# Another order of the same work in a three-layer fp32 block kernel

## The reference, cut to what matters

```python
# first block: one layer, no feed-forward
h = rms(x, norm_w) @ w_in                      # 1024 -> 3584
oa = diff_attention(rms(qa), rms(ka), va)      # 4 heads, two 64-wide maps each, softmax, w = p0 - lam * p1
orr = rms(retention_fwd + retention_bwd)       # 4 heads, decay masks, chunks of 128
x = x + concat(rms(oa) * silu(ga), orr * silu(gr)) @ w_out
# second block, layer 0: bidirectional mLSTM with 4 heads; layer 1: window attention, 16 query heads, 4 kv heads, rope
x = x + mixer(rms(x)) ; x = x + (silu(h @ Wg) * (h @ Wu)) @ Wd      # feed-forward width 2816
return rms(x) * norm_final_w
```

## Time and profile before

| | us |
|---|---|
| median of 3 runs | 1539.77 |
| lowest, highest | 1539.58, 1541.7 |
| the profiled execution | 1538.49 |
| its span (first to last instruction) | 1536.7 |
| PE busy | 1455.4 |
| DVE, ACT, POOL busy | 800.9, 595.0, 52.8 |
| mean granted TensorE clock | 0.976 |

### The profile page before, as it was taken

One profiled execution on the slowest core, in us unless ns is written; L12 is line 12 of the kernel. 1 busy time (PEld: TensorE's weight loads), 2 busy tenths in 40 slices (PEclk: granted clock), 3 DMA queues, 4 the chain that ended last, 5 costly groups with the idle time before them and its releaser, 6 DMA issues.

```text
span 1536.7 us, 17599 instructions
## 1 busy us (share of the span) xinstructions
PE 1455.4 (95%) x6854; PEld 1170.2 (76%) x6854; DVE 800.9 (52%) x1640; ACT 595.0 (39%) x1201; POOL 52.8 (3%) x108
## 2 busy tenths in 40 slices
PE   8988999989999889999999999998899999999998
PEld 7765775778777767888888888766568888888887
DVE  5455564356656645554345545577555544344533
ACT  6554443235335424332223323366553332232322
POOL 0101000000000000000000000001000000000000
PEclk9998999999999999999999999999899999999999
DMA  5311011022221103222333222321103232232222
GB/s 209 110 55 55 24 59 55 28 96 100 96 69 69 55 28 110 87 105 76 107 113 104 82 93 95 113 71 42 62 28 110 82 103 89 96 110 89 86 96 73
DMA packets 25922, 127.98 MB, mean 83 GB/s; under 512 B 3248, under 2 KB 5936, under 8 KB 14832
## 3 DMA queue, kind: packets, MB, share of 16 engines
q1 hardware_dynamic: 25408, 126.60, 24.4%
q10 hardware_dynamic: 432, 0.27, 0.1%
HBM read 122.01 MB, written 2.23 MB: 81 GB/s over the span
## 4 chain that ended last, share of the span: by engine, by line
PE 81%; DVE 9%; ACT 6%; issue 2%; DMA 1%; POOL 1%; SPq 0%; DVEq 0%; POOLq 0%; ACTq 0%
PE PS L558 79%; DVE WL L1161 2%; ACT WH L901 1%; PE PS L819 1%; ACT FT L901 1%; DVE FT L1167 1%; POOL SC L1659 1%; PE PS L577 1%; DVE FT L1161 1%; DVE FT L1164 1%; DVE FR L1161 1%; DVE FT L1597 1%; ACT FT L904 1%; DVE G L1161 1%; ACT L901 1%
## 5 line engine op out<-in xcount | busy, mean ns | idle before, releaser
L1161 DVE TENSOR_TENSOR WL<-RAW,WH 128x512 fp32r<-128x512 f32 (+1 forms) x454 | 294.5, 673 | 302.1 <-ACT WH L901 301.4
L558 PE MATMUL PS<-XH,WH 128*128 128x512 f32 x1080 | 435.8, 404 | 1.6 <-DVE WL L1161 1.2
L558 PE MATMUL PS<-XH,WL 128*128 128x512 f32 x1080 | 423.3, 392 | 0.0
L558 PE MATMUL PS<-XL,WH 128*128 128x512 f32 x1080 | 423.0, 392 | 0.0
L558 PE MATMUL PS<-FR,WH 128*128 128x512 f32 (+1 forms) x1132 | 346.0, 389 | 19.4 <-DVE WL L1161 14.2
L901 ACT ACTIVATE WH<-RAW 128x512 fp32r<-128x512 f32 (+1 forms) x454 | 256.1, 607 | 178.9 <-PE PS L558 176.4
L558 PEld LDWEIGHTS PS<-FR,WH 128*128 128x128 f32 x1132 | 212.4, 192 | 64.1 <-DVE WL L1161 12.8
L558 PEld LDWEIGHTS PS<-XH,WH 128*128 128x128 f32 x1080 | 204.0, 189 | 53.1 <-issue 9.1
L558 PEld LDWEIGHTS PS<-XH,WL 128*128 128x128 f32 x1080 | 204.2, 189 | 43.9
L558 PEld LDWEIGHTS PS<-XL,WH 128*128 128x128 f32 x1080 | 204.4, 189 | 41.4 <-issue 1.7
L558 PE MATMUL PS<-FR,WL 128*128 128x512 f32 (+1 forms) x566 | 218.3, 386 | 0.0
(11 more groups left out here) (120 smaller groups left out, 1188.7 us busy)
## 6 DMA issues: line engine op xcount, KB each, us to landing
RAW<-in_f_in SPq DMA_DIRECT2D x44, 1024.0 KB, 4.9
RAW<-in_w_in SPq DMA_DIRECT2D x12, 1024.0 KB, 4.8
RAW<-in_m_in SPq DMA_DIRECT2D x12, 1024.0 KB, 5.0
RAW<-in_f_oa SPq DMA_DIRECT2D x16, 768.0 KB, 4.2
RAW<-in_f_ob SPq DMA_DIRECT2D x16, 640.0 KB, 3.9
RAW<-in_a_in SPq DMA_DIRECT2D x6, 1024.0 KB, 4.9
RAW<-in_w_out SPq DMA_DIRECT2D x4, 1024.0 KB, 4.9
RAW<-in_m_out SPq DMA_DIRECT2D x4, 1024.0 KB, 4.8
```

The source lines that it names most:

```text
L558: return e.matmul(o, l, r, start=start, stop=stop, skip_group_check=True)
L1161: return e.tensor_tensor(o, a, b, op)
```

## The change

Three things change, and one wait is added. The number and kind of matmuls, splits, evictions, loads and side units is the same.

1. `units()` lists a step's splits ahead of its evictions; before they stood behind them.
2. In `out_stage` the step of k = 7 becomes one step for each of the first tiles. Each tile is then done, and its eviction listed, one by one. The release of part 3 of the two chunks comes with the last tile that reads it.
3. A table `SHIFT` moves 291 of the 449 side units by -6 to +11 steps; a half step orders units within a step. The `rr` units now start from the moved places of `rq`.
4. DVE's part of `pa` waits until the product two units before is made, since `pa` and `pb` can now stand in another order.

```diff
+SHIFT = {
...
+    ("mix", 10): 1.5, ("mix", 11): 1, ("mix", 12): 5, ("mix", 13): 7, ("mix", 15): 1, ("mix", 17): 1, ("mix", 19): 5,
...
+    ("op", 1, 1): 1, ("op", 1, 2): 1, ("op", 1, 3): 2, ("op", 2, 0): 1.5, ("op", 2, 1): 1, ("op", 2, 2): 1,
+    ("op", 2, 3): 1, ("op", 3, 0): 1, ("op", 3, 1): 0.5, ("pa", 0, 0): 0.5, ("pa", 0, 2): 2, ("pa", 1, 0): -1.5,
...
+    ("pb", 3, 0): -2, ("pb", 3, 1): -2, ("pb", 3, 2): 2, ("pv", 0): -3, ("pv", 1): 0.5, ("pv", 2): -2, ("qk2", 0): 1,
+    ("qk2", 1): 0.5, ("qk2", 2): 2.5, ("qk2", 3): -0.5, ("qk2", 5): -0.5, ("qk2", 6): 0.5, ("qk2", 7): 3.5,
...
+}
...
     def side(self, at, *units):
-        self.sides.setdefault(at, []).extend(units)
+
+        for u in units:
+            self.places[u] = at + SHIFT.get(u, 0)
...
     def units(self):
-        out = []
+        out, sides = [], {}
+        for u in sorted(self.places, key=self.places.get):
+            sides.setdefault(int(self.places[u]), []).append(u)
         for i, (pe, ev, w) in enumerate(self.steps):
-            out += [pe, *ev, *w, *self.sides.get(i, ())]
+            out += [pe, *w, *ev, *sides.get(i, ())]
...
-        for k in range(KT):
-            P.step(("o1", ts, k), [j, j + 1], k // 2 if k % 2 else None)
-        for t in ts:
-            P.tiles[t].done = len(P.steps)
-        P.ev(*[("ev", t) for t in ts])
+        for k in range(KT - 1):
+            P.step(("o1", ts, ts, k), [j, j + 1], k // 2 if k % 2 else None)
+        for d, t in enumerate(ts):
+            P.tiles[t].done = P.step(("o1", ts, [t], KT - 1), [j, j + 1])
+            P.release[j + d // 2, 3] = len(P.steps)
+            P.ev(("ev", t))
...
                 a = acol[:, kt * 64 + 32 * d + hd:kt * 64 + 32 * d + hd + 1]
+                p.wait_ge("pg", 2 * (n - 2) + d + 1)
                 tri = CO[:, K_TF:K_TF + 128] if d == 0 else CO[:, K_TB:K_TB + 128]
```

More of the change, by code:

```diff
@@ L37 @@
          "mk": "mkl", "mg": "mgev", "rope": "rope1", "o": "xadd", "fg": "fg", "fu": "fu", "dn": "xadd"}
+SHIFT = {
[13 rows of a table added]
+    ("mix", 2): 5.5, ("mix", 3): 2, ("mix", 5): 1.5, ("mix", 6): 1, ("mix", 7): 2, ("mix", 8): 2, ("mix", 9): -1,
+    ("mix", 10): 1.5, ("mix", 11): 1, ("mix", 12): 5, ("mix", 13): 7, ("mix", 15): 1, ("mix", 17): 1, ("mix", 19): 5,
+    ("mix", 20): -2.5, ("mix", 21): -0.5, ("mix", 22): -0.5, ("mix", 23): -0.5, ("mt", 0, 0): 1.5, ("mt", 0, 1): 3.5,
[23 rows of a table added]
+    ("tab", 3): 2, ("tab", 4): 1.5, ("tab", 5): 1, ("tab", 6): -3, ("tab", 7): -5, ("tab", 8): -6, ("tab", 9): 5.5,
+    ("tab", 10): 6, ("tab", 11): 11, ("tab", 12): 8, ("tab", 13): 6, ("tn", 0): -0.5, ("tn", 1): -1, ("tn", 3): 1,
[4 rows of a table added]
+}
 class Prog:
@@ L64, in __init__ @@
         self.steps, self.begin, self.release, self.group = [], {}, {}, {}
-        self.misc, self.sides = {}, {}
+        self.misc, self.places = {}, {}
     def chunk(self, ap, nk, width):
@@ L411, in make_plan @@
     o2 = out_stage(16, 79, (0, 1, 7))
[L412 to L416, removed]
+    seen = {u[1]: int(at) for u, at in P.places.items() if u[0] == "rq"}
     for x, i in seen.items():
@@ L638, in mixed, with o1 @@
                        k == 0, k == KT - 1)
-        def o1(ts, k):
+        def o1(every, ts, k):
             base = tiles[ts[0]].base
@@ L643, in o1 @@
                 p.wait_ge(*{0: ("scev", 48), 8: ("pg", 32), 16: ("mdv", P.misc["nb", 3] + 1)}[base])
-                for t in ts:
+                for t in every:
                     bank_free(t)
             p.wait_ge("mxl", base + k + 1)
-            p.wait_ge("wl", wl(tiles[ts[0]].j, k))
-            p.wait_ge("wl", wl(tiles[ts[0]].j + 1, k))
+            p.wait_ge("wl", wl(tiles[every[0]].j, k))
+            p.wait_ge("wl", wl(tiles[every[0]].j + 1, k))
             for t in ts:
```

## The result

The changed kernel takes 1456.35 us, the median of 4 runs (1450.82 to 1457.49), against 1539.67 before on the same chips: a ratio of 0.9453, interval 0.9424 to 0.9482.

A forecast was written before the change was run, and what follows sets the result against it. TensorE's 81.3 us of idle time and its lowered clock were taken as the room: 16.5 + 13 + 6 + 11.3 + 9.3 = 56.1 us, less 10 for unseen waits, so 46 off, 1494 us; range 1472 to 1524.

The forecast's parts named there:

- the signs that the forecast named: No output-stage wait over 1 us, clock near 1.00; slow matmuls in about 7 places, not 16; idle near 50 us.
- Output stages: Two four-tile output stages: waits of 0.78 and 5.99 us go in each; 13.5 idle + 4.0 clock - 1 = 16.5 us.
- I allow 10 us beyond those named: Whole kernel: 10 us charged for the new order's own waits, which the trace could not show, with 291 units moved.
- the 2 + 2 + 2 + 1 us of named new waits: Losses: transpose behind sums 2, head 3's numerators 2, units ahead of output-stage splits 2, chunk 17's first split 1.
- The transpose two steps behind its sums: Differential attention (31:158): one transpose gets two steps instead of three behind its column sums; may cost 2 us.
- the numerators of head 3: mLSTM (318:561): two numerators now one step (1.4 us) apart, charged 2 us.
- the third output stage: After window attention: eleven units stand in its first step ahead of splits its third step needs, charged 2 us.
- the fifth score unit's: Differential attention: its 4.4 us wait behind a low split; unit moves back 1.5 steps, 3.4 us taken to go.
- "60%": Differential attention (31:158): share of the 7.8 us clock cost taken to come back, 4.7 us.
- Splits ahead of evictions elsewhere: Outside the four-tile output stages: evictions move back 1.3 us; cost between 0 and 44 us, taken as 0.
- The rival of stalled banks: Evictions behind splits stall the two-bank stages at 34 tile ends: up to 44 us, slower at 1567; chance 6%.
- "All fits": Rival: no new waits, named losses of 7 us don't come; 1539.8 - 73 = 1467 at far end, about 1473 middle; 17%.

The follow-up runs named there:

- three stage tables: Changed kernel with the table cut to one stage's side units: first block 1484.42 us, mLSTM 1494.71, window attention 1491.71; without any table 1507.79.
- the probe: Changed kernel with thirteen waits of TensorE for GpSimd powers put into the second feed-forward: 1505.15 us, ratio 0.9776, 51 us over the changed kernel.

## Why the prediction was wrong

- **Direction and mechanism were right.** The idle time bounded the kernel, the matmuls' own work was untouched, and the waits that the forecast named did go. The first feed-forward is unchanged at 369.9 us between the same instructions. Of the signs that the forecast named, the output stages show theirs (no wait over 1 us, the split of chunk 16 between two adds); the others went further than said: 3 slow places instead of about 7, 24.4 us idle instead of near 50.
- **Output stages: right.** 17.5 us against 16.5. The tight place was seen rightly: the first split of chunk 17 is done at 280.9, 0.7 us before its tile begins. That either edit would do nearly all of it alone was not seen: the forecast told their effects as a sum.
- **The failed step is the charges against the sum:** "I allow 10 us beyond those named", with the 2 + 2 + 2 + 1 us of named new waits. Of these 17 us some 6 came, the new waits listed above. The transpose two steps behind its sums waits for nothing; the numerators of head 3 have one wait of 0.7, not 2 more; the third output stage has 4.3 us of idle time where it had 8.8. I had taken the unknown as cost on one side only. The three stage tables show that the stages' shifts don't lean on each other.
- **Second, waits kept that went.** The first score unit (1.1), the transposes behind a head's norm (1.4), the rest of the fifth score unit's and the last pair's were taken to stay, since they did not move away from their producers. With the table alone the first two indeed stay (0.95 and 1.56 us); with the splits first as well they go. In all some 16 us of idle time more than forecast went at the old places.
- **Third, the busy time: 26.2 us came back instead of 16.5.** Half of the surplus is clock, 21.4 us instead of 16.5: "60%", "35%" and the like took the clock to follow the idle time, but the long waits, which the lower clock mostly stands behind, were the ones that went. The other half, 4.8 us, had no term in the forecast: TensorE's busy time also holds some 0.2 us for each wait at the full clock.
- **Splits ahead of evictions elsewhere: 0 was taken, between 0 and 44.** In the changed kernel they are worth 6 us in favour. The rival of stalled banks showed in one place: the first projection tile waits 0.86 instead of 0.34 us for its bank, while the 1.24 us wait for a weight part three steps on is gone.
- **The likeliest rival was the first, "All fits", and it too stopped short,** at 1467 at the far end, since it took no more clock than the forecast's. Its own sum doesn't come out either: 56.1 and the 7 us of named losses are 63, so 1477. The 73 has the blanket 10 us in it, which the 56.1 never held.

In sum: 11 us of charges that didn't come, 16 of kept waits that went, 5 of clock and 4.8 of busy time around waits are 36.9 us, which is 83.1 less the forecast's 46.2.

## What to carry to other kernels

When one engine bounds a kernel and its idle time sits in short waits, ask for each wait whether unit and producer can be put apart, and count with it the slow clock behind it and the 0.2 us around it; a blanket charge for waits that no row shows is as much a guess as a gain would be (here 6 of 17 us came). Two edits that relieve the same wait must be summed as one. And list first what the bounding engine wants soonest, ahead of an eviction with time to spare: in a queue worked off in order this costs the eviction a microsecond, and took away waits of the first block's mixers here, 7.5 us.

## What was not expected of the hardware

In the probe short waits of TensorE (1.2 to 1.4 us, even four of them 6.9 us apart) left its matmuls at 0.39 us, while one of 2.49 us was followed by 3.4 us of matmuls at 0.63. In the mixers two waits of 1.1 us that start 1.7 us apart lowered the clock, and so did a single one of 1.35 us. Over all traces the share of waits with the lower clock behind them rises from 12 of 83 under 1.8 us to 30 of 31 over 2.6: the second and third microsecond of a wait are dearer than the first. The slow work didn't grow in step with the wait: 3.4, 3.4, 5.6 and 4.4 us behind 2.49, 3.89, 5.09 and 7.22.
